# Prompt attention: exponentials read the statistics tile, ScalarE copies the results

## The chip, the cores and the metric

The kernel runs on one core of a Trainium2 chip. The metric is the device time of one execution in microseconds (us). The engines are TensorE (PE in the profile, PEld for its weight loads), VectorE (DVE), ScalarE (ACT), GpSimd (POOL) and SyncE (SP, which here only issues transfers).

## The reference

One layer of a hybrid decoder for a prompt of 2048 tokens and 8 sample sequences of 8 tokens. What matters here is the softmax attention of the prompt: three groups of 4 heads (head size 64), with dilations 1, 4 and 16; each query sees itself and 128 positions back at its group's stride.

```
s = q k^T / 8 - slope * distance        (masked outside the window)
m = max(s);  p = exp(s - m);  den = sum(p)
o = p v                                  (not yet divided)
```

`m` and `den` are needed later, when the groups are combined with weights equal to their denominators. Before this stage come the projections of the whole input, after it the attention of the samples, a chunked delta rule, two output projections and a layer norm.

## The kernel before

The program is written out engine by engine with semaphores. `attend_prompt` does the prompt attention in 48 units: 3 groups g, each with 16 blocks of 128 queries. A unit has two pairs p of heads, each with two heads h. `x.kb` says over how many blocks of keys a unit runs: 2 in the first group and in three of four units of the second, 1 in the third group and for blocks with no predecessor. In group two tokens are taken with a step of 4, in group three with a step of 16, both in q and k as read by TensorE and in the result tile `att_T` as written.

`schedule` gives every engine the same order of steps; step k handles unit k+1 (`nxt`), k (`now`) and k-1 (`prev`):

- TensorE: `score(nxt)` into `ps_s`; `weigh(prev)`, probabilities times values into `ps_o`, after `t_read` of each pair p and after `o_read` of the unit before; then `transpose(now)` into `ps_t`.
- VectorE: `turn(prev)` copies the transposed probabilities of pair 0 to `probs_T`; `maxima(nxt)` adds the bias, writes `scores` and takes the row maximum into `top` (L1321); two small multiplications by -1 write `neg` (L1326) and `stats` (L1327); `results(prev)` copies `ps_o` to `att_T` (L1332) and posts `o_read`.
- ScalarE: `turn(prev)` for pair 1 (L1367), then `exps(nxt)`: four exponentials with `neg` as bias and the row sum into `stats` (L1361), after `neg_put`.
- SyncE loads the groups' tiles, stores finished rows of `att_T` after `o_read`, and the statistics.

There is one `ps_o` and one `probs_T`, two slots of `scores`, `probs` and `neg`. `att_T` of groups one and three is the same tile; hence a wait for `row_stored[0]` (group one's stores) before group three writes it. In the trace the result tile of group two goes by the name `v_first`, whose place it takes.

The stage after, `attend_samples`, starts on ScalarE with a table load and the activations of the gates (L1770 to L1775); VectorE builds the decay rates from them, and TensorE adds these up (L1577) before it scores the second half of the samples (L1518).

Of the kernel before, what the change touches and what calls it, by code (L numbers as in the profile page):

```python
# [8 lines left out]
ALU = mybir.AluOpType  # L9
# [3 lines left out]
P = 128  # L13
# [9 lines left out]
HPG, DH = 4, 64  # L23
# [1017 lines left out]
def attend_prompt(nc, t, block, first, late, pair, g_last):  # L1041


    with ExitStack() as ctx:
# [12 lines left out]
        probs = sb("probs", [P, 2, NP_, 2, 2 * P])  # L1057
        probs_T = sb("probs_T", [P, NP_, 4, P])
        top = sb("top", [P, HPG])
        neg = sb("neg", [P, 2, HPG])  # L1060
        turnstile = sb("turnstile", [P, NP_])
        ps_s = [[pb(f"ps_s{p}{h}", [P, 512]) for h in range(2)] for p in range(NP_)]
        ps_t = [pb(f"ps_t{p}", [P, 4, P]) for p in range(NP_)]
# [3 lines left out]
        qk_in = [sem(f"qk_in{g}") for g in range(NG)]  # L1067
        v_in = [sem(f"v_in{g}") for g in range(NG)]
        stat_put = sem("stat_put")
        neg_put, o_full, o_read = sem("neg_put"), sem("o_full"), sem("o_read")  # L1070
        s_full = [sem(f"s_full{p}") for p in range(NP_)]
        s_read = [sem(f"s_read{p}") for p in range(NP_)]
        exp_done = [sem(f"exp_done{p}") for p in range(NP_)]
# [231 lines left out]
        @block.vector  # L1305
        def _(dve):
            dve.wait_ge(bias0_in, 16)

            def maxima(x):
                for p in range(NP_):  # L1310
                    dve.wait_ge(s_full[p], x.u + 1)
                    if x.after(2):
                        dve.wait_ge(exp_done[p], 2 * (x.u - 1))
                    if x.after(1):
                        dve.wait_ge(stat_put, x.u)

                    dve.memset(turnstile[:, p:p + 1], 0.0)
                    for h in range(2):
                        head = 2 * p + h
                        off = 2 * P - P * x.kb  # L1320
                        dve.tensor_tensor_reduce(out=scores[:, x.slot, p, h, 0:P * x.kb], in0=ps_s[p][h][:, 0:P * x.kb],  # L1321
                                                 in1=bias[x.g][:, head, off:], scale=DH ** -0.5, scalar=-3.0e38, op0=ALU.add,
                                                 op1=ALU.max, accum_out=top[:, head:head + 1]).then_inc(s_read[p], 1)
                for p in range(NP_):
                    dve.wait_ge(s_read[p], 2 * (x.u + 1))
                dve.tensor_scalar(neg[:, x.slot, :], top[:, :], -1.0, None, ALU.mult).then_inc(neg_put, 1)  # L1326
                dve.tensor_scalar(stats[:, x.g, x.b:x.b + 1, 0:HPG], top[:, :].unsqueeze(1), -1.0, None,  # L1327
                                  ALU.mult).then_inc(stat_put, 1)

            def results(x):  # L1330
                dve.wait_ge(o_full, x.u + 1)
                dve.tensor_copy(x.tokens(att_T[x.g], 0), ps_o[:, :, :]).then_inc(o_read, 1)  # L1332

            def step(nxt, now, prev):
                if prev:
                    turn(dve, lambda o, i: dve.tensor_copy(o, i), 0, prev)
                if nxt:
                    maxima(nxt)
                if prev:
                    results(prev)  # L1340

            def enter(g):
                if g == 2:
                    dve.wait_ge(row_stored[0], 16 * 4)

            def leave(g):
                if g == 0:
                    dve.wait_ge(bias_in, 16)
            schedule(step, enter, leave=leave)

        @block.scalar
        def _(act):

            def exps(x):
                act.wait_ge(neg_put, x.u + 1)
                for p in range(NP_):
                    if x.after(2):
                        act.wait_ge(t_full[p], x.u - 1)
                    for h in range(2):
                        head = 2 * p + h  # L1360
                        act.activation(probs[:, x.slot, p, h, 0:P * x.kb], scores[:, x.slot, p, h, 0:P * x.kb], ACT.Exp,  # L1361
                                       bias=neg[:, x.slot, head:head + 1],
                                       accum_out=stats[:, x.g, x.b:x.b + 1, HPG + head]).then_inc(exp_done[p], 1)

            def step(nxt, now, prev):
                if prev:
                    turn(act, lambda o, i: act.activation(o, i, ACT.Copy), 1, prev)  # L1367
                if nxt:
                    exps(nxt)
            schedule(step)  # L1370


CACHED = sum(KEPT)
# [2786 lines left out]
```

## Time and profile before

| | us |
|---|---|
| median of 3 runs | 2448.22 |
| lowest, highest | 2446.05, 2450.98 |
| span of the profiled execution | 2441.7 |
| TensorE busy in the span | 2332.4 |
| VectorE busy | 1644.5 |
| ScalarE busy | 1165.6 |
| prompt attention, from to | 1414.0 to 1571.7 |

The profiled execution is one run of its own; the profile gives its span, from the first to the last instruction, and no other time for it. What lies around the span is therefore known only as the difference between the median and the span, 6.5 us. In a row of the timeline the first number is the start in us from the span's start, the second the length of the row (which may hold several instructions), and the bracket at its end is the idle time of that engine before it and what ended it; "issue" is a wait for nothing that the profile shows.

### The profile page before, as it was taken

The page shows a single profiled execution, that of the slowest core. Times are in us where ns is not written, and L with a number is a line of the kernel's source. Part 1 is how long each engine was busy: PE and PEld are TensorE (multiplying, and loading weights), DVE is VectorE, ACT ScalarE, POOL GpSimd, SP SyncE. Part 2 cuts the span into 40 slices and gives each one's busy share as a digit, 9 for nine tenths or more (in the row PEclk, how much of TensorE's full clock was granted, in tenths as well). Part 3 has the DMA queues.
Part 4 walks back from the last instruction along what each step waited for, and adds up shares of the span by engine and source line. Part 5 has one row for each costly group of instructions (what it writes and reads, how often), then busy time and mean ns, then how long its engine had stood idle before and what let it go on. Part 6 is the DMA issues. An engine that isn't in the chain of part 4 may idle for free. (4 is left out here: it accounts for less than half of the span.)

```text
span 2441.7 us, 45441 instructions
## 1 busy us (share of the span) xinstructions
PE 2332.4 (96%) x16842; PEld 2056.4 (84%) x16842; DVE 1644.5 (67%) x4158; ACT 1165.6 (48%) x2458; POOL 375.0 (15%) x628
## 2 busy tenths in 40 slices
PE   5999999999999999999999999979999899999998
PEld 2777788888899999999999966648888699999786
DVE  5867676554363776776644467758996877677897
ACT  4444444444431543544444466737776533333454
POOL 0000000000111111110000000222322035345100
PEclk8999999999999999999999999979999699999999
DMA  7232323333532323323333363876666566657563
GB/s 264 95 113 95 113 96 112 104 105 100 192 99 87 93 92 109 98 87 110 108 107 108 109 247 122 306 251 176 164 179 196 175 201 194 200 183 237 184 215 128
DMA packets 246588, 363.59 MB, mean 149 GB/s; under 512 B 48598, under 2 KB 180286, under 8 KB 241120
## 3 DMA queue, kind: packets, MB, share of 16 engines
q1 hardware_dynamic: 187792, 224.11, 29.8%
q0 software_dynamic: 36560, 125.17, 13.4%
q10 hardware_dynamic: 22016, 11.40, 1.7%
q8 instruction: 135, 2.21, 0.4%
q14 instruction: 85, 0.70, 0.1%
HBM read 246.94 MB, written 113.68 MB: 148 GB/s over the span
## 5 line engine op out<-in xcount | busy, mean ns | idle before, releaser
L310 PE MATMUL ps_f<-m_lo,w_hi 128*128 128x272 f32 (+1 forms) x2436 | 789.6, 324 | 13.5 <-DVE m_lo L620 6.9
L310 PE MATMUL ps_f<-m_hi,w_hi 128*128 128x272 f32 (+1 forms) x2436 | 793.4, 326 | 0.0
L310 PE MATMUL ps_f<-m_hi,w_lo 128*128 128x272 f32 (+1 forms) x2436 | 784.7, 322 | 0.0
L310 PEld LDWEIGHTS ps_f<-m_lo,w_hi 128*128 128x128 f32 x2436 | 458.8, 188 | 68.4 <-issue 33.0
L310 PEld LDWEIGHTS ps_f<-m_hi,w_lo 128*128 128x128 f32 x2436 | 459.6, 189 | 36.8
L310 PEld LDWEIGHTS ps_f<-m_hi,w_hi 128*128 128x128 f32 x2436 | 458.7, 188 | 33.7
L684 DVE TENSOR_TENSOR stage<-partial,ps_f 128x512 f32<-128x512 f32 (+2 forms) x348 | 171.4, 506 | 319.0 <-PE ps_f L310 307.5
L435 ACT ACTIVATE partial<-ps_f 128x272 f32<-128x272 f32 (+1 forms) x348 | 161.1, 463 | 392.6 <-PE ps_f L310 390.9
L397 ACT ACTIVATE w_hi<-w_raw 128x512 fp32r<-128x512 f32 x348 | 213.0, 625 | 204.0 <-PE ps_f L310 128.1
L591 DVE TENSOR_TENSOR w_lo<-w_raw,w_hi 128x512 fp32r<-128x512 f32 x348 | 239.1, 688 | 85.0 <-ACT w_hi L397 81.5
L709 DVE SCALAR_TENSOR_TENSOR conv<-stage,side,conv 128x1024 f32<-128x1024 f32 x108 | 138.3, 1281 | 8.1 <-ACT conv L451 6.9
L65 PE MATMUL ps_f<-wv_lo,m_hi 128*128 128x256 f32 (+1 forms) x384 | 109.4, 285 | 4.2 <-DVE wv_lo L751 3.7
L66 PE MATMUL ps_f<-wv_hi,m_lo 128*128 128x256 f32 (+1 forms) x384 | 109.6, 286 | 0.0
L67 PE MATMUL ps_f<-wv_hi,m_hi 128*128 128x256 f32 (+1 forms) x384 | 109.0, 284 | 0.0
L1361 ACT ACTIVATE probs<-scores,neg 128x256 f32<-128x256 f32 (+1 forms) x192 | 86.3, 450 | 45.2 <-DVE neg L1326 45.2
L66 PE MATMUL ps_fm<-u_hi,w_tail_lo 128*128 128x256 f32 (+1 forms) x336 | 97.2, 289 | 0.0
L66 PE MATMUL ps_fm<-u_first_hi,w_tail_lo 128*128 128x256 f32 x336 | 95.0, 283 | 0.0
L898 POOL DMA_DIRECT2D scratch_conv_d<-conv x36 | 19.5, 540 | 431.0 <-ACT conv L457 424.3
L65 PEld LDWEIGHTS ps_f<-wv_lo,m_hi 128*128 128x128 f32 x384 | 73.4, 191 | 4.8 <-DVE wv_lo L751 4.1
L457 ACT ACTIVATE conv<-conv 128x1024 f32<-128x1024 f32 (+1 forms) x36 | 39.1, 1086 | 78.4 <-DVE conv L709 50.6
L67 PEld LDWEIGHTS ps_f<-wv_hi,m_hi 128*128 128x128 f32 x384 | 73.6, 192 | 0.0
L66 PEld LDWEIGHTS ps_f<-wv_hi,m_lo 128*128 128x128 f32 x384 | 73.3, 191 | 0.0
(766 smaller groups left out, 4783.1 us busy)
## 6 DMA issues: line engine op xcount, KB each, us to landing
w_raw<-in_w_feat SPq DMA_DIRECT2D x58, 1024.0 KB, 5.9
gates<-scratch_g_d SPq DMA_DIRECT2D x56, 256.0 KB, 3.2
m_rows<-scratch_parts_d SPq DMA_DIRECT2D x16, 768.0 KB, 5.0
z_f<-scratch_z_d ACTq DMA_DIRECT2D x13, 768.0 KB, 6.7
scratch_conv_d<-conv POOLq DMA_DIRECT2D x18, 544.0 KB, 3.0
scratch_conv_d<-conv POOLq DMA_DIRECT2D x18, 512.0 KB, 2.9
kc<-in_k_cache SPq DMA_DIRECT2D x8, 1152.0 KB, 15.1
vc<-in_v_cache POOLq DMA_DIRECT2D x8, 1152.0 KB, 16.3
```

Of the source, the lines that this page charges most:

```text
L65: pe.matmul(out, ah, bl, start=start, stop=False)
L66: pe.matmul(out, al, bh, start=False, stop=False)
L67: return pe.matmul(out, ah, bh, start=False, stop=stop)
L310: last = pe.matmul(out[:, 0:n], l[:, cols], r, start=start and k == 0 and nth == 0, stop=k == KH - 1 and nth == 2, skip_group_check=not start)
L397: act.activation(wh[j][:, :], source(q, j), ACT.Copy).then_inc(w_hi_done[j], 1)
L435: act.activation(f[:, which, 0:n], src[:, 0:n], ACT.Copy).then_inc(put, 1)
L457: act.activation(conv[:, j, 0:n], conv[:, j, 0:n], ACT.Silu).then_inc(conv_silu, 1)
L591: put(dve.tensor_tensor(wl[j][:, :], source(q, j), f32(wh[j][:, :]), ALU.subtract), w_lo_done[j])
L684: last = dve.tensor_tensor(x[:, S_PRE + HT * h + at:S_PRE + HT * h + at + m], left[:, 0:m], right[:, 0:m], ALU.add)
L709: put(dve.scalar_tensor_tensor(out=conv[:, j, 0:PT], in0=x[:, n:n + PT], scalar=w, in1=conv[:, j, 0:PT], op0=ALU.mult, op1=ALU.add), conv_ ...
L898: pool.dma_start(t["conv_d"][tile(q, j), :, PT * s:PT * s + n], conv[:, j, 0:n]).then_inc(conv_stored[j], 16)
L1361: act.activation(probs[:, x.slot, p, h, 0:P * x.kb], scores[:, x.slot, p, h, 0:P * x.kb], ACT.Exp, bias=neg[:, x.slot, head:head + 1], acc ...
```

## The change

The tile `neg` and its semaphore go. The exponentials wait for `stat_put` and take their bias from `stats`. `results`, with its wait for `o_full`, moves from VectorE's step to the end of ScalarE's step, and with it the wait for `row_stored[0]` before group three.

```diff
-        neg = sb("neg", [P, 2, HPG])
...
-                dve.tensor_scalar(neg[:, x.slot, :], top[:, :], -1.0, None, ALU.mult).then_inc(neg_put, 1)
                 dve.tensor_scalar(stats[:, x.g, x.b:x.b + 1, 0:HPG], top[:, :].unsqueeze(1), -1.0, None,
                                   ALU.mult).then_inc(stat_put, 1)
-
-            def results(x):
-                dve.wait_ge(o_full, x.u + 1)
-                dve.tensor_copy(x.tokens(att_T[x.g], 0), ps_o[:, :, :]).then_inc(o_read, 1)
...
-                if prev:
-                    results(prev)
-
-            def enter(g):
-                if g == 2:
-                    dve.wait_ge(row_stored[0], 16 * 4)
...
-            schedule(step, enter, leave=leave)
+            schedule(step, leave=leave)
 
         @block.scalar
         def _(act):
 
             def exps(x):
-                act.wait_ge(neg_put, x.u + 1)
+                act.wait_ge(stat_put, x.u + 1)
...
-                                       bias=neg[:, x.slot, head:head + 1],
+                                       bias=stats[:, x.g, x.b, head:head + 1],
                                        accum_out=stats[:, x.g, x.b:x.b + 1, HPG + head]).then_inc(exp_done[p], 1)
 
             def step(nxt, now, prev):
...
                 if nxt:
                     exps(nxt)
-            schedule(step)
+                if prev:
+                    results(prev)
+
+            def results(x):
+                act.wait_ge(o_full, x.u + 1)
+                act.activation(x.tokens(att_T[x.g], 0), ps_o[:, :, :], ACT.Copy).then_inc(o_read, 1)
+
+            def enter(g):
+                if g == 2:
+                    act.wait_ge(row_stored[0], 16 * 4)
+            schedule(step, enter)
```

## Rows read from the trace of the kernel before

**Rows 1.** Busy time by head group: stretch, length, engines' busy us, clock.

```profile
1414.00:1467.70 53.70, 52.14 (x468) 37.16 (x468) 42.44 (x223) 40.50 (x143) 0.00 (x0) 0.94 0.74 281
1467.70:1531.00 63.30, 63.30 (x500) 44.45 (x496) 45.42 (x239) 41.08 (x156) 0.00 (x0) 1.00 0.34 128
1531.00:1571.70 40.70, 38.14 (x324) 27.32 (x321) 30.55 (x211) 29.72 (x137) 5.88 (x14) 1.00 0.91 325
```

**Rows 2.** Timeline, first group: start us, length us, engine, work.

```profile
1442.17 0.51 ACT L1361 ACTIVATE probs<-scores,neg 128x256 f32<-128x256 f32 x1 [0.93 <-DVE neg L1326]
...
1444.16 0.57 ACT L1367 ACTIVATE probs_T<-ps_t 128x512 f32<-128x512 f32 x1
...
1444.78 0.42 PEld L1261 LDWEIGHTS ps_o<-probs_T,v_first 128*64 128x64 f32 x8 [0.40 <-ACT probs_T L1367]
...
1445.37 0.86 PEld L1250 LDWEIGHTS ps_t<-ident_top,probs 128*128 128x128 f32 x8 [0.17 <-issue]
...
1446.39 0.73 PEld L1237 LDWEIGHTS ps_s<-k_first,q_first 64*128 64x128 f32 x8 [0.17 <-issue]
...
1447.15 0.42 DVE L1321 CUSTOM_DVE_ANT_0 scores<-ps_s,bias_head 128x256 f32<-128x256 f32 x1 [0.40 <-issue]
...
1448.73 0.17 DVE L1326 TENSOR_SCALAR neg<-top 128x4 f32<-128x4 f32 x1
1448.81 0.16 DVE L1327 TENSOR_SCALAR stats<-top 128x4 f32<-128x4 f32 x1
...
1448.93 0.51 ACT L1361 ACTIVATE probs<-scores,neg 128x256 f32<-128x256 f32 x1 [0.93 <-DVE neg L1326]
```

**Rows 3.** Timeline, third group.

```profile
1534.93 0.40 ACT L1361 ACTIVATE probs<-scores,neg 128x128 f32<-128x128 f32 x1 [0.86 <-DVE neg L1326]
...
1536.90 0.20 PEld L1261 LDWEIGHTS ps_o<-probs_T,v_sb 128*64 128x64 f32 x4 [0.39 <-ACT probs_T L1367]
...
1539.95 0.40 ACT L1361 ACTIVATE probs<-scores,neg 128x128 f32<-128x128 f32 x1 [0.78 <-DVE neg L1326]
```

**Rows 4.** Timeline, second group.

```profile
1494.03 0.57 ACT L1367 ACTIVATE probs_T<-ps_t 128x512 f32<-128x512 f32 x1
...
1494.57 0.85 PEld L1261 LDWEIGHTS ps_o<-probs_T,v_first 128*64 128x64 f32 x16 [0.70 <-issue]
...
1497.77 0.57 ACT L1367 ACTIVATE probs_T<-ps_t 128x512 f32<-128x512 f32 x1
1497.85 0.96 PEld L1261 LDWEIGHTS ps_o<-probs_T,v_first 128*64 128x64 f32 x16 [0.22 <-issue]
```

**Rows 5.** VectorE's result copy: durations ns min/median/max, groups one, two, three.

```profile
L1332 DVE COPY att_T<-ps_o x15: 417/425/426, 1421.8 to 1469.0; 128x256 f32<-128x256 f32 x15
...
L1332 DVE COPY v_first<-ps_o x16: 611/630/647, 1477.0 to 1532.4; 128x256 f32<-128x256 f32 x16
...
L1332 DVE COPY att_T<-ps_o x16: 579/589/597, 1534.9 to 1571.8; 128x256 f32<-128x256 f32 x16
```

**Rows 6.** ScalarE's turn of 128x256: busy us, mean ns, idle before.

```profile
L1367 ACT ACTIVATE probs_T<-ps_t 128x256 f32<-128x256 f32 x21 | 7.6, 363 | 1.1 <-PE ps_t L1250 1.1
```

**Rows 7.** Timeline, two ScalarE copies in a row, next stage.

```profile
1608.52 0.60 ACT L1812 ACTIVATE o_rows_s<-ps_so 128x512 f32<-128x512 f32 x1 [12.45 <-PE ps_so L1554]
1609.01 0.38 ACT L1813 ACTIVATE o_rows_s<-ps_so 128x256 f32<-128x256 f32 x1
```

**Rows 8.** Timeline, the seam to the next stage.

```profile
1571.13 1.28 ACT L1770 ACT_TABLE_LOAD   x1
...
1571.84 0.60 DVE L1332 COPY att_T<-ps_o 128x256 f32<-128x256 f32 x1 [0.84 <-PE ps_o L1261]
...
1577.22 0.30 PEld L1577 LDWEIGHTS ps_G<-coef,tri_incl 128*128 128x128 f32 x2 [0.84 <-issue]
...
1579.49 0.77 PE L1518 MATMUL ps_ss<-k_new,q_bd_s 128*128 128x64 f32 x5 [0.44 <-DVE top_s L1636]
```

**Rows 9.** Busy time in the stage after; columns as in rows 1.

```profile
1587.00:1648.00 61.00, 46.01 (x321) 30.32 (x319) 31.49 (x159) 20.49 (x66) 15.49 (x22) 0.76 0.73 251
```

More of the change, by code:

```diff
@@ L1069, in attend_prompt @@
         stat_put = sem("stat_put")
-        neg_put, o_full, o_read = sem("neg_put"), sem("o_full"), sem("o_read")
+        o_full, o_read = sem("o_full"), sem("o_read")
         s_full = [sem(f"s_full{p}") for p in range(NP_)]
```

## The prediction

> **What bounds the kernel now.** I read the profile from the stage that is changed outwards: first the busy times of the three head groups of the prompt attention, then the chain inside one pair of units in each group, then the seam to the next stage. A unit is one block of 128 queries with 4 heads; there are 48, 16 in each group.
>
> The stage lasts 157.7 us, from 1414.0 to 1571.7, and TensorE is busy nearly all of it; VectorE and ScalarE are each busy about three quarters [rows 1]. That alone would say that a copy may move freely between the two. It is the wrong reading here, because busy TensorE time is pipelined and the question is who releases its next instruction.
>
> In the first group follow one lap [rows 2]. ScalarE starts the exponentials of a unit at 1442.17. After the four of them (1.99 us) it copies half of the transposed probabilities of the unit before (`turn`, L1367) from 1444.16. TensorE's second half of `weigh` waits for that copy, and its weights load at 1444.78, behind an idle 0.40 that ScalarE ends. Then come the transposes (1445.37), the scores of the unit after next (1446.39), VectorE's scaled maxima (1447.15, after 0.40 of idling), the negated maximum (1448.73), and ScalarE again at 1448.93. So the lap takes 6.76 us and carries the even units; the odd ones make the same lap in between. Two units per 6.76 us is 3.38 us a unit, and 16 of them are 54 us, which is the length of the first group [rows 1]. So this ring of latencies sets the pace, and ScalarE's stretch "exponentials, then turn" lies on it without a gap. VectorE lies on it only between its first maximum and the negation; everything else it does falls into time in which it then idles.
>
> In the third group it is the same with shorter tiles: 1534.93 to 1539.95, 5.02 us for two units, with a visible wait of 0.39 for ScalarE's turn [rows 3].
>
> The second group reads its queries and keys with a stride, its score matmuls take longer, and there TensorE's own work sets the pace: it loads weights at 1494.57 without a wait for ScalarE, whose turn is over at 1494.60 [rows 4]. The second half of `weigh` begins some 0.43 later, at 1495.00, so ScalarE has 0.40 to spare. Once in each row of four units the scores are short (a block with no predecessor), and there the turn ends at 1498.34 where the second half would start at 1497.85 + 0.43 = 1498.28: nothing to spare [rows 4].
>
> **The change part by part.**
>
> *One multiplication less on VectorE.* Today `neg` is written at 1448.73 and the same values to `stats` at 1448.81, 0.08 later [rows 2]. After the change the `stats` write comes first and the exponentials wait for it. It takes 0.16 us against 0.17 for `neg`, so ScalarE starts when it did. Gain on the ring: 48 times 0.01 at most, taken as zero. The 0.08 saved behind it is VectorE time ahead of an idle 0.40.
>
> *The result copy leaves VectorE.* It took 0.42 us a unit in the first group, 0.63 in the second and 0.59 in the third [rows 5]. It ran after the negation, while ScalarE was in its exponentials, and was followed by VectorE's turn and then idling before the next maximum. It was on no ring, so its removal gives nothing. If that cover were gone it would be worth 16 x (0.42 + 0.63 + 0.59) = 26 us, but other engines hold the pace long before (rival 2).
>
> *The result copy joins ScalarE, behind the exponentials of the unit after next and ahead of the next turn.* The semaphore it waits for (`o_full`) is up by then: TensorE is past `weigh` at 1445.37, and the exponentials that begin about then take 1.99 us [rows 2]. So it does not wait. But it is queued in front of exactly the copy for which TensorE waits in groups one and three. No row shows this copy on ScalarE. The nearest is its turn of the same 128 x 256 shape from PSUM, 0.36 us [rows 6]. That row writes contiguous rows. In groups two and three the destination steps by 4 and by 16 elements, and there VectorE pays 0.63 - 0.42 = 0.21 and 0.59 - 0.42 = 0.17 more than in group one [rows 5]. I take the same extra for ScalarE: 0.36, 0.57, 0.53. Two ScalarE copies in a row overlap: one of 0.60 us starts at 1608.52 and the next at 1609.01, so 0.11 of each is hidden [rows 7]. What the turn is put back by is then 0.25, 0.46 and 0.42 us.
>
> The ScalarE page of the Trainium skill (ScalarE: Activation LUTs, section "What ACT_TABLE_LOAD costs") gives 186 ns + 0.833 ns an element, 0.40 us here, and an overlap of 93 ns; the turn's 0.36 [rows 6] and the overlap of 0.11 [rows 7] are a little better. By the page each delay would be 0.06 larger, which over the 20 delays below is 1.2 us more. The skill's page on SBUF (SBUF — State Buffer, section "Door 1: The DMA port swizzle") says that accesses which go to a new 16-byte line each time pay a penalty, whatever engine makes them; VectorE's 0.63 and 0.59 agree [rows 5], ScalarE's share is shown by no row. Without any such penalty the sum would be 6.0 instead of 8.3.
>
> Now the sum. First group: the ring of 6.76 grows by 0.25 for every two units, 8 x 0.25 = 2.0 us. Third group: 8 x 0.42 = 3.4 us. Second group: of the four steps of a row only the one with short scores is bare, 4 x 0.46 = 1.8 us; in the others the 0.40 to spare covers most of 0.46, and a delay in one step gives the next one more room. Together 7.2 us. The other new wait, TensorE's first half of `weigh` for `o_read`, now posted by ScalarE at the end of the copy, is met at about the moment at which the turn starts; the first half takes 0.43 and the turn 0.57, so the turn still ends last.
>
> *The seam.* Today ScalarE leaves the stage with its last turn and starts a table load for the next stage at 1571.13, while VectorE copies the last result from 1571.84, when TensorE has finished it [rows 8]. After the change ScalarE must do that copy first, and the load starts near 1571.84 + 0.53 - 0.11 = 1572.26, 1.1 us later against TensorE. Behind it hang the gate exponentials of the next stage, VectorE's work on them, and TensorE, which already idles 0.84 at 1577.22 and 0.44 for VectorE's maxima at 1579.49 [rows 8]. So the 1.1 is passed on. *The wait for `row_stored`* moves from VectorE to ScalarE ahead of group three: group one is over at 1467.7 and group three begins at 1531.0 [rows 1], so stores that follow each row of group one have had 63 us, and it waits for nothing. If they were late, the turns would be held. SyncE's stores of the results wait for `o_read`, which comes up to 2 us later in a unit; nothing reads them before the stage after.
>
> Sum: 7.2 + 1.1 = 8.3 us. The profiled span is 2441.7 us and the median of the three times 2448.2, so 6.5 us lie around the span; I leave them as they are. 2448.2 + 8.3 = 2456.5 us, 0.34% slower. A measurement of this kernel can tell about 0.2% (4.9 us) from no change.
>
> Bounds. Below: no extra for strides, 20 x 0.25 = 5.0 and a covered seam: 2453.2. Above: ScalarE copies in VectorE's times with no overlap, and the ordinary steps of group two show 0.63 - 0.40 once a row: 8 x 0.42 + 4 x 0.86 + 8 x 0.59 + 1.3 = 12.8, giving 2461.0.
>
> **The rivals.**
>
> *Rival 1, it is hidden (same).* The waits for ScalarE are small (0.40, of which 0.17 is also shown where nothing is waited for, and 0.39) [rows 2, 3]. If a queue inside TensorE is the true limit and the ring only looks closed, only the seam is left: 2449.3. Against it: the laps of 6.76 and 5.02 close without a gap.
>
> *Rival 2, VectorE was the pace (not slower).* If the maxima started when VectorE got to them, freeing it would pull the ring in, until TensorE is without waits: 0.40 - 0.17 = 0.23 per pair in group one and 0.39 in group three, 8 x 0.23 + 8 x 0.39 = 5.0 us, so 2443.2 at best. It decides only if VectorE's idle 0.40 ahead of L1321 is not there; the row shows it [rows 2].
>
> *Rival 3, TensorE's clock falls otherwise in the next stage (faster or much slower).* From 1587 to 1648 the granted clock averages 0.76, so for 0.24 / 0.5 x 61 = 29 us the engine is at 1.2 GHz and not 2.4; it is busy in only 46 of the 61 us there [rows 9]. Work that arrives some 8 us later could meet fewer low stretches: if all were gone and TensorE's work there were bare, 15 us come back and the end is 2456.5 - 15 = 2441.5. As well it can meet more of them, and with 10 us more the end is 2466. For it: nothing ties those stretches to our work but its gaps. Against: the gaps are made by that stage's own chain and move with it.
>
> *Rival 4, strided PSUM to SBUF copies are dearer on ScalarE than on VectorE.* Well above 0.40 + 0.11 us group two is exposed in its ordinary steps too: at 1.0 us it is 2.0 + 4 x 0.9 + 12 x 0.5 + 8 x 0.9 + 1.5 = 20 us, 2468. No row speaks for so much.
>
> **How the numbers follow.** Forecast 0.68; rival 1 0.17; faster, by the clock or by rival 2 with the scatter of runs, 0.06; rivals 3 and 4 on the slow side 0.09. The range reaches from rival 1's 2449.5 to a little over the upper bound, 2463.5, which leaves 2 in 10 out; the forecast's own range is 2453 to 2461. Slower by over 0.2%: nearly all of the forecast but its lowest edge, and the slow side of 3 and 4, 0.74. Within 0.2%: rival 1 and that edge, 0.20. Faster 0.06.
>
> **What would show it.** In the profile after: the copy stands between the fourth exponential and the turn, at 0.36, near 0.57 and near 0.53 us; two laps of group one take about 7.0 us and of group three about 5.45; TensorE's wait for ScalarE (or for the copy itself) ahead of `weigh` grows; VectorE idles over 0.8 us a unit; the table load follows the last copy, and TensorE's idle 0.84 at the sums of the gate grows to nearly 2. I am wrong if the laps keep their length, if the copy waits for `o_full`, or if the stage is about 7 us longer and the end does not move.

## The result and the profile after

The changed kernel takes 2453.6 us, the median of 10 runs (2450.8 to 2458.8); the kernel before took 2446.6 us in the 10 runs beside it (2442.0 to 2451.0). The ratio is 1.0032, with an interval of 1.0022 to 1.0041: 0.32% slower, where 0.34% was forecast. Against the median of 2448.2 that the forecast started from, 2456.5 was put at 8.3 us more; against the 2446.6 of the larger sample the ratio gives 7.8 us.

Wherever a run's time stands beside its span, little lies around the span: 1.8 to 1.9 us in the kernel before, 1.7 to 1.8 in the changed kernel, up to 2.2 in some of the runs below. The profiled execution of the kernel before was thus a short one (2441.7 + 1.8 = 2443.5), not one of median length with 6.5 us around it. The spans of the two profiled executions differ by 10.8 us, more than the medians. So I compare the stage, which repeats, and not the spans.

The first group after the change, in the timeline (start, length, engine, work, idle time before and its end):

```profile
1440.81 0.51 ACT L1348 ACTIVATE probs<-scores,stats 128x256 f32<-128x256 f32 x1 [0.93 <-DVE stats L1324]
...
1442.79 0.36 ACT L1362 ACTIVATE att_T<-ps_o 128x256 f32<-128x256 f32 x1
...
1443.06 0.58 ACT L1354 ACTIVATE probs_T<-ps_t 128x512 f32<-128x512 f32 x1
1443.20 0.90 PEld L1260 LDWEIGHTS ps_o<-probs_T,v_first 128*64 128x64 f32 x16 [0.93 <-ACT att_T L1362]
...
1444.27 0.86 PEld L1249 LDWEIGHTS ps_t<-ident_top,probs 128*128 128x128 f32 x8 [0.17 <-issue]
...
1445.30 0.73 PEld L1236 LDWEIGHTS ps_s<-k_first,q_first 64*128 64x128 f32 x8 [0.17 <-issue]
...
1446.06 0.42 DVE L1319 CUSTOM_DVE_ANT_0 scores<-ps_s,bias_head 128x256 f32<-128x256 f32 x1 [0.40 <-issue]
...
1447.84 0.51 ACT L1348 ACTIVATE probs<-scores,stats 128x256 f32<-128x256 f32 x1 [0.93 <-DVE stats L1324]
```

Beside [rows 2] the reader sees the copy of 0.36 us at 1442.79, behind the fourth exponential, and the turn 0.27 later. The lap from exponentials to exponentials is 1447.84 - 1440.81 = 7.03 us; it was 6.76. TensorE's idle before `weigh` is 0.93 and named after the copy itself: it waits for `o_read` at the first half, and the second half no longer waits at all (16 weights in one row). VectorE's step now begins its maxima where it did, relative to the scores.

The third group, against [rows 3]; the lap is 5.47 us and was 5.02:

```profile
1542.29 0.40 ACT L1348 ACTIVATE probs<-scores,stats 128x128 f32<-128x128 f32 x1 [0.37 <-DVE stats L1324]
...
1543.85 0.57 ACT L1362 ACTIVATE att_T<-ps_o 128x256 f32<-128x256 f32 x1
...
1544.24 0.40 ACT L1354 ACTIVATE probs_T<-ps_t 128x256 f32<-128x256 f32 x1
...
1544.48 0.42 PEld L1260 LDWEIGHTS ps_o<-probs_T,v_sb 128*64 128x64 f32 x8 [0.59 <-ACT att_T L1362]
...
1547.76 0.40 ACT L1348 ACTIVATE probs<-scores,stats 128x128 f32<-128x128 f32 x1 [0.37 <-DVE stats L1324]
```

A unit with short scores in the second group, against [rows 4]; the copy takes 0.60 and TensorE, which did not wait there, is idle for 0.78:

```profile
1498.06 0.60 ACT L1362 ACTIVATE v_first<-ps_o 128x256 f32<-128x256 f32 x1
...
1498.45 0.63 ACT L1354 ACTIVATE probs_T<-ps_t 128x512 f32<-128x512 f32 x1
...
1498.71 0.85 PEld L1260 LDWEIGHTS ps_o<-probs_T,v_first 128*64 128x64 f32 x16 [0.78 <-ACT v_first L1362]
```

The seam, against [rows 8]:

```profile
1574.60 0.42 PEld L1260 LDWEIGHTS ps_o<-probs_T,v_sb 128*64 128x64 f32 x8 [1.79 <-ACT att_T L1362]
...
1576.82 1.41 PEld L1515 LDWEIGHTS ps_ss<-k_new,q_bd_s 128*128 128x128 f32 x12 [0.17 <-issue]
...
1576.93 0.60 ACT L1362 ACTIVATE att_T<-ps_o 128x256 f32<-128x256 f32 x1 [0.67 <-PE ps_o L1260]
1577.54 1.28 ACT L1767 ACT_TABLE_LOAD   x1
...
1583.38 0.30 PEld L1574 LDWEIGHTS ps_G<-coef,tri_incl 128*128 128x128 f32 x2 [1.92 <-issue]
...
1585.44 2.33 PEld L1515 LDWEIGHTS ps_ss<-k_new,q_bd_s 128*128 128x128 f32 x12 [0.42 <-DVE top_s L1633]
```

ScalarE copies the last result at 1576.93 and loads its table at 1577.54, 0.72 us behind TensorE's first score of the samples (1576.82); before it was 0.60 ahead of it (1571.13 against 1571.7). TensorE's idle at the sums of the gate is 1.92 us and was 0.84.

The laps and three lengths tell the kernels apart; all are differences of starts in the timelines. "Exponentials" is the time from the first exponential of unit 0 to that of unit 47, "stage" that from TensorE's first score to its first score of the samples, "seam" that from there to the sums of the gate.

| kernel | lap, group 1 | row of 4 units, group 2 | lap, group 3 | exponentials | stage | seam | time against before (interval) |
|---|---|---|---|---|---|---|---|
| before | 6.76 | 15.03 | 5.03 | 151.4 | 157.7 | 5.5 | |
| after | 7.03 | 15.60 | 5.46 | 158.3 | 164.9 | 6.6 | 1.0032 (1.0022 to 1.0041) |
| neg removed only | 6.76 | 15.03 | 5.03 | 151.1 | 158.0 | 5.6 | 0.9997 (0.9981 to 1.0013) |
| copy moved only | 7.03 | 15.60 | 5.46 | 158.2 | 165.1 | 8.3 | 1.0040 (1.0026 to 1.0053) |
| VectorE relieved, ScalarE not loaded | 6.76 | 15.02 | 5.03 | 151.4 | 159.1 | 5.6 | 0.9998 (0.9987 to 1.0009) |
| after, last two copies on VectorE | 7.03 | 15.60 | 5.46 | 158.3 | 165.9 | 9.0 | 1.0040 (1.0026 to 1.0054) |
| after, one more small copy | 7.11 | 15.78 | 5.55 | 160.1 | 166.8 | 6.7 | one run |
| after, contiguous writes | 7.04 | 15.30 | 5.30 | 156.1 | 163.7 | 6.4 | 1.0026 (1.0014 to 1.0038) |
| after, copy ahead of exponentials | 7.18 | 15.35 | 5.66 | 160.7 | 167.9 | 8.8 | 1.0056 (1.0039 to 1.0072) |
| both turns on VectorE | 6.22 | 14.92 | 4.67 | 144.7 | 155.3 | 7.8 | 0.9985 (0.9971 to 0.9999) |
| the same, samples' queries early | 6.22 | 14.92 | 4.66 | 144.3 | 149.6 | 5.5 | 0.9971 (0.9960 to 0.9983) |
| before, samples' queries early | 6.76 | 15.04 | 5.02 | 151.1 | 157.4 | 5.5 | 0.9994 (0.9983 to 1.0005) |

### The profile page after: what moved, and what is told of

Same layout as the page of the kernel before. It is cut to its first block and busy times, and to the rows that moved or that the text cites. A ratio compares the mean times of both kernels' runs of the same rounds, so it can differ in the third digit from the quotient of the medians.

```text
span 2452.5 us, 45393 instructions
## 1 busy us (share of the span) xinstructions
PE 2340.2 (95%) x16842; PEld 2062.7 (84%) x16842; DVE 1622.8 (66%) x4062; ACT 1184.0 (48%) x2506; POOL 374.0 (15%) x628
## 5 line engine op out<-in xcount | busy, mean ns | idle before, releaser
L1348 ACT ACTIVATE probs<-scores,stats 128x256 f32<-128x256 f32 (+1 forms) x192 | 86.3, 450 | 35.0 <-DVE stats L1324 34.9
L987 DVE TENSOR_TENSOR sub_prod<-sub_u,sub_w 96x60 f32<-96x60 f32 (+34 forms) x434 | 71.7, 203 | 4.0 <-issue 3.6
## 6 DMA issues: line engine op xcount, KB each, us to landing
vc<-in_v_cache POOLq DMA_DIRECT2D x8, 1152.0 KB, 17.5
```

Of the source, the lines that this page charges most:

```text
L987: dve.tensor_tensor(prod[:, rows, 0:m], u[:, i:i + 1, i + 1:].broadcast_to(some), w[:, rows, i:i + 1].broadcast_to(some), ALU.mult).then_i ...
```

## The experiments

### One half each: which edit costs

The first run takes the tile `neg` away and leaves the copy on VectorE:

```diff
-                dve.tensor_scalar(neg[:, x.slot, :], top[:, :], -1.0, None, ALU.mult).then_inc(neg_put, 1)
...
-                act.wait_ge(neg_put, x.u + 1)
+                act.wait_ge(stat_put, x.u + 1)
...
-                                       bias=neg[:, x.slot, head:head + 1],
+                                       bias=stats[:, x.g, x.b, head:head + 1],
```

> The kernel before with one edit only: the tile neg and its multiplication are gone and the exponentials read the statistics tile; VectorE still copies the results. My theory (the ring of latencies): the statistics are written at the moment at which neg was, so nothing moves: two laps of group one stay 6.76 us, of group three 5.02, the stage 157.7 us, the time within 0.1% of before. The rival (VectorE's instructions count one by one): 48 x 0.08 us less, the stage near 154 us.

Measured: laps of 6.76 and 5.03 us, exponentials 151.1 us, ratio 0.9997. The first edit is worth nothing, as its place ahead of an idle VectorE says.

The second run keeps `neg` and moves `results` and the wait for `row_stored[0]` to ScalarE, as in the changed kernel.

> The other half alone: ScalarE copies the results behind the exponentials, neg stays. My theory: the whole loss is here; the stage is as long as with both edits, 164.9 us (before 157.7), laps 7.03 and 5.47 us, and the time about 7 us above before. The rival (the later statistics tile costs something, or the two edits work against each other): the stage differs from 164.9 by over 1 us.

Measured: 7.03 and 5.46 us, stage 165.1, ratio 1.0040. Every lap is that of the changed kernel. The whole loss is in the move of the copy.

### VectorE without the copy, ScalarE without it

```diff
-                dve.tensor_copy(x.tokens(att_T[x.g], 0), ps_o[:, :, :]).then_inc(o_read, 1)
+                if x.u == 0:
+                    dve.wait_ge(att_clear, 1)
+                n = P if x.g == 1 else 2
+                dve.tensor_copy(x.tokens(att_T[x.g], 0)[:, :, 0:n], ps_o[:, :, 0:n]).then_inc(o_read, 1)
```

> VectorE is relieved and ScalarE is not loaded: as the run with neg removed, but in groups one and three VectorE copies 2 of 128 columns of each result, so the results of these groups are left out (GpSimd clears their tile once at the start of the stage; group two copies in full). My theory (VectorE's copy lies under ScalarE's exponentials): the stage stays 157.7 us within 1 us. The rival (VectorE was the pace): the laps of groups one and three shrink by up to 0.23 and 0.39 us, the stage is up to 5 us shorter.

The laps do not move (6.76, 5.03), the exponentials take 151.4 us as before, and the ratio is 0.9998. In the timeline of this run the short copy is followed by a turn that waits for TensorE:

```profile
1440.87 0.16 DVE L1335 COPY att_T<-ps_o 128x4 f32<-128x4 f32 x1
...
1441.36 0.69 DVE L1339 COPY probs_T<-ps_t 128x512 f32<-128x512 f32 x1 [0.34 <-PE ps_t L1251]
```

The 0.42 us taken away from VectorE came back as waiting for the transposes and for the scores. The stage, expected within 1 us of 157.7, is 1.4 us longer, but not in the laps: 1.3 of it lie ahead of the first exponential, where one write of the statistics takes 1.45 us while GpSimd's added clearing runs. So rival 2 is out: VectorE was not the pace, and its relief was worth nothing to begin with.

### The price per ScalarE time

```diff
+                act.activation(junk[:, :], ps_o[:, 0, 0:32], ACT.Copy)
                 act.activation(x.tokens(att_T[x.g], 0), ps_o[:, :, :], ACT.Copy).then_inc(o_read, 1)
```

> The changed kernel with one more small ScalarE copy (128 x 32 from the same PSUM tile to a spare tile) ahead of each result copy. My theory (every bit of ScalarE time between exponentials and turn is paid once per lap in groups one and three and once per row of four in group two): about 0.1 us of queue time x 20 delays, so the stage goes from 164.9 to about 167 us, a little more if the ordinary steps of group two are bare by now. The rival (ScalarE idles 0.4 to 0.9 us a unit and takes it for nothing): 164.9.

A lap grows by 0.08 and 0.09 us, a row by 0.18, the exponentials by 1.8 us and the stage by 1.9. That is 8 x 0.08 + 8 x 0.09 + 4 x 0.18 = 2.1 us by the laps. A row of group two pays 0.18, twice the price and not once, as if two of its steps were bare with the copy in them. (Its one time, 2453.0 us, cannot tell 2 us.)

```diff
-                act.activation(x.tokens(att_T[x.g], 0), ps_o[:, :, :], ACT.Copy).then_inc(o_read, 1)
+                act.activation(att_T[x.g][:, :, P * x.b:P * (x.b + 1)], ps_o[:, :, :], ACT.Copy).then_inc(o_read, 1)
```

> The changed kernel, but ScalarE writes each result to contiguous columns of its tile and not with the group's step, so the results of groups two and three lie in the wrong columns. My theory: the copy takes 0.36 us in all groups instead of 0.61 and 0.58; laps of group three near 5.3 us instead of 5.47, rows of group two 0.4 us shorter; the stage about 162.8 us. The rival (the longer copies come from reading PSUM while TensorE works with long strided matmuls, not from the step of the write): 0.6 us remain and 164.9.

The copy's durations (ns, min/median/max, groups one and three, then group two):

```profile
L1362 ACT ACTIVATE att_T<-ps_o x32: 357/362/386, 1423.4 to 1577.4; 128x256 f32<-128x256 f32 x32
L1362 ACT ACTIVATE v_first<-ps_o x16: 359/362/363, 1480.5 to 1536.3; 128x256 f32<-128x256 f32 x16
```

With contiguous writes every copy takes 0.36 us, where the changed kernel's took 0.60 in group two and 0.58 in group three. So the step of the write is what costs, 0.24 and 0.22 us a copy, and the rival (TensorE's strided matmuls) is out. Laps of group three shrink from 5.46 to 5.30 and rows of group two from 15.60 to 15.30: the exponentials take 156.1 us, 2.2 less. The stage is 163.7 us, 0.9 over what was expected of it; that part lies behind the last exponentials (5.4 us from there to the samples' scores, 4.4 in the changed kernel), where the granted clock is 0.50 from 1574 to 1577 and was 1.00 in the changed kernel.

### Another place for the copy on ScalarE

```diff
+                if prev:
+                    results(prev)
                 if nxt:
                     exps(nxt)
-                if prev:
-                    results(prev)
```

> The changed kernel with ScalarE's result copy ahead of the exponentials of its step and not behind them. There ScalarE idles 0.45 to 0.93 us before, so a count of idle time says: hidden, the stage is near 158 us. My theory says no: the copy must wait for the weighing, which waits for ScalarE's turn, so a ring of one step closes: turn 0.57 + weighing 0.65 + copy 0.27 + exponentials 1.98 = 3.5 us a unit in group one (as now) and 0.36 + 0.45 + 0.49 + 1.55 = 2.85 in group three (2.73 now): the stage about 166 us, not shorter than the changed kernel.

The idle time ahead of the exponentials was no free place: the ratio is 1.0056, the laps 7.18 and 5.66 us, and the stage 167.9 us, 2 more than expected. In group three one reads the ring of one step: weights after the turn, copy after the weighing, exponentials after the copy, turn after the exponentials:

```profile
1545.62 0.37 ACT L1354 ACTIVATE probs_T<-ps_t 128x256 f32<-128x256 f32 x1
...
1546.04 0.20 PEld L1260 LDWEIGHTS ps_o<-probs_T,v_sb 128*64 128x64 f32 x4 [0.52 <-ACT probs_T L1354]
...
1546.53 0.60 ACT L1362 ACTIVATE att_T<-ps_o 128x256 f32<-128x256 f32 x1 [0.54 <-PE ps_o L1260]
...
1546.94 0.36 ACT L1348 ACTIVATE probs<-scores,stats 128x128 f32<-128x128 f32 x1
...
1548.46 0.36 ACT L1354 ACTIVATE probs_T<-ps_t 128x256 f32<-128x256 f32 x1
```

The turn starts at 1545.62, the copy at 1546.53 and the next turn at 1548.46: the ring closes in 2.84 us a unit, half of 5.66. Group two, paced by TensorE, is indeed a little better off here (15.35 against 15.60).

### The seam alone

```diff
+                if prev and prev.u >= 46:
+                    dve.wait_ge(o_full, prev.u + 1)
+                    dve.tensor_copy(prev.tokens(att_T[prev.g], 0), ps_o[:, :, :]).then_inc(o_read, 1)
...
-                if prev:
+                if prev and prev.u < 46:
                     results(prev)
```

> The changed kernel with the copies of the last two units given back to VectorE. My theory of the seam: ScalarE's table load for the next stage starts 1.1 us earlier against TensorE, and from the end of the last weighing to TensorE's sums of the gate it is 5.5 us again and not 6.6; the stage itself keeps 164.9 us less some tenths. The rival (the seam is set by something else): 6.6 us remain. Whether the 1.1 us reach the end of the kernel is open: in the profile of the changed kernel the stage behind had given them back some 65 us later; if so, the time is that of the changed kernel.

```profile
1577.21 1.28 ACT L1770 ACT_TABLE_LOAD   x1
1578.00 2.63 PEld L1518 LDWEIGHTS ps_ss<-k_new,q_bd_s 128*128 128x128 f32 x12 [0.33 <-issue]
...
1578.11 0.59 DVE L1334 COPY att_T<-ps_o 128x256 f32<-128x256 f32 x1 [1.30 <-PE ps_o L1260]
...
1587.02 0.30 PEld L1577 LDWEIGHTS ps_G<-coef,tri_incl 128*128 128x128 f32 x2 [0.84 <-issue]
```

The table load comes 0.79 us ahead of the samples' scores again, and TensorE's idle at the sums is 0.84 again: this much of the mechanism of the seam is as described. But the length came out at 9.0 us and not 5.5, for a reason that neither theory had: here TensorE runs at the lower clock. (A later run, with both turns on VectorE as well, has the same last two copies at a clock of 1.00, and there the seam is 5.5 us.) Twelve weight loads took 2.63 us, where the changed kernel's took 1.41. In its profile, in that with only the copy moved (8.3 us) and in that with the copy ahead (8.8 us), the granted clock falls to 0.50 at the seam. In this profile TensorE has just idled 1.79 us before the weighing of unit 46, where it must wait for a copy that stands behind the last four exponentials, and 0.55 before that of 47. The first wait is new; the changed kernel has it too. In the changed kernel's own profile the clock held at the seam and fell right behind it (2.33 us for the next twelve weights at 1585.44). Whether the 1.1 us of the seam reach the end could not be told from the times: 1.0040 against the changed kernel's 1.0032, with intervals that overlap.

The starts of VectorE's instructions tell how far it goes, if they are counted from the stage's first score and not from the start of the span, from which that score lies 0.5 to 2.2 us less far in these profiles than in the one before (1414.1). The instruction that starts at 1597 before is then 10.2 us late with only the copy moved, 6.7 with contiguous writes and 11.7 with the last copies on VectorE; stage and seam together are 10.2, 6.9 and 11.7 us longer. So as far as 1597 the seam is passed on whole, within 0.3 us. In the changed kernel's profile the same count gives 11.4 us where stage and seam make 8.4. The other 3.0 us fall where its granted clock is 0.50, from about 1586 to 1592; in the kernel before it is 1.00 from 1571 to 1597.

### Opening the ring

If ScalarE's stretch "exponentials, copy, turn" is the ring, then ScalarE may have the copy if it loses the turn.

```diff
                     turn(dve, lambda o, i: dve.tensor_copy(o, i), 0, prev)
+                    turn(dve, lambda o, i: dve.tensor_copy(o, i), 1, prev)
...
-                if prev:
-                    turn(act, lambda o, i: act.activation(o, i, ACT.Copy), 1, prev)
+                if prev:
+                    results(prev)
                 if nxt:
                     exps(nxt)
-                if prev:
-                    results(prev)
```

> The changed kernel with both turns on VectorE, and ScalarE's result copy ahead of its exponentials. My theory: this opens the ring, because the exponentials no longer have a turn behind them; TensorE's own 3.27 and 2.33 us a unit are left: laps of 6.54 and 4.66 us, the stage 4 to 5 us shorter than before, 153 to 154.5 us, and the time some 0.15% below before. The rival (VectorE, at two turns and the maxima some 3.1 us a unit, becomes the pace, or its later maxima close another ring): the stage 158 us or longer.

```profile
1441.73 0.68 DVE L1330 COPY probs_T<-ps_t 128x512 f32<-128x512 f32 x1
...
1442.34 0.42 DVE L1319 CUSTOM_DVE_ANT_0 scores<-ps_s,bias_head 128x256 f32<-128x256 f32 x1
...
1442.52 0.85 PEld L1260 LDWEIGHTS ps_o<-probs_T,v_first 128*64 128x64 f32 x16 [0.33 <-issue]
...
1443.66 0.39 ACT L1361 ACTIVATE att_T<-ps_o 128x256 f32<-128x256 f32 x1 [0.56 <-PE ps_o L1260]
...
1443.91 0.17 DVE L1324 TENSOR_SCALAR stats<-top 128x4 f32<-128x4 f32 x1
1444.12 0.51 ACT L1349 ACTIVATE probs<-scores,stats 128x256 f32<-128x256 f32 x1
```

Now the weights of `weigh` load 16 in a row with nothing before them but the 0.33 of changing from scores, ScalarE is idle before its copy, and VectorE goes from turn to maxima without a pause. The lap of group one is 6.22 us, less than the 6.54 that I had called TensorE's own: that figure still held the gap between the two halves of `weigh`. Together the exponentials take 144.7 us, 6.7 less than before. But the stage is only 2.4 us shorter (155.3, where 153 to 154.5 was expected), and the timeline says why:

```profile
1564.79 4.95 POOL L1221 TENSOR_SCALAR q_bd_s<-q_s 64x64 f32<-64x64 f32 x12 [34.97 <-DMA bias_s<-in_bias_samples]
...
1569.79 2.64 PEld L1514 LDWEIGHTS ps_ss<-k_new,q_bd_s 128*128 128x128 f32 x12 [5.47 <-POOL q_bd_s L1221]
```

TensorE arrived 5.47 us before GpSimd had the samples' queries in place, and that work (4.95 us) had waited for the last of five small loads. It had always ended near there; in the kernel before TensorE happened to come 0.3 us behind it. The next run lets GpSimd start as soon as the queries themselves have landed, and gives the last two copies to VectorE:

```diff
-                sp.dma_start(late["q_in"][:, :, :], ...).then_inc(late["small_in"], 16)
+                sp.dma_start(late["q_in"][:, :, :], ...).then_inc(late["q_landed"], 16)
...
-            pool.wait_ge(late["small_in"], 80)
+            pool.wait_ge(late["q_landed"], 16)
...
             pe.wait_ge(q_put, 1 + 4 * NG)
+            pe.wait_ge(small_in, 64)
```

> The kernel with both turns on VectorE and the copy ahead of the exponentials, with two more edits: VectorE copies the results of the last two units, and GpSimd prepares the samples' queries as soon as these have landed (a semaphore of their own) and not after all five small loads, for which TensorE waits itself. In the run before this one the stage's laps were 6.7 us shorter in sum but TensorE then waited 5.2 us for GpSimd's product, which stood behind the last of those loads. My theory: with that wait gone the stage keeps its gain, about 151 us from the first score to the first score of the samples (before 157.6), no idle time for GpSimd's tile, TensorE's idle at the sums of the gate 0.84 as before; the time 5 to 7 us below before. The rival: the samples' keys and the bias land late as well, so another wait, for a transfer, takes the place, and the gain stays at 2 to 3 us.

```profile
1562.69 1.42 PEld L1518 LDWEIGHTS ps_ss<-k_new,q_bd_s 128*128 128x128 f32 x12 [0.17 <-issue]
...
1568.18 0.30 PEld L1577 LDWEIGHTS ps_G<-coef,tri_incl 128*128 128x128 f32 x2 [0.84 <-issue]
```

The wait is gone (0.17 before the samples' weights), the stage is 149.6 us, the seam 5.5, and the time 2439.9 us against 2446.2: ratio 0.9971, interval 0.9960 to 0.9983. It beats both kernels. The same edit alone, beside the removal of `neg`:

> The kernel before without neg, and with GpSimd's early preparation of the samples' queries alone. There GpSimd was ready 0.3 us before TensorE came, so my theory gives nothing: stage 157.6 us, time as before within 0.1%. If it gains, that wait was on the path already.

Stage 157.4 us, ratio 0.9994: nothing, as expected. The gain belongs to the open ring, and the early queries only let it pass.

### Where the lead of the faster kernel goes

The stage is 8.1 us shorter, the time 6.3, and the one profiled execution is not shorter at all (span 2442.7). To see where a lead goes I take the starts of the same VectorE instructions in two profiles. The table gives how much later (+) or earlier (-) than in the profile of the kernel before they start, each counted from the start of its span; its columns are the start there, to a few us.

| kernel | 1597 | 1618 | 1672 | 1895 | 1988 | 2006 | 2398 |
|---|---|---|---|---|---|---|---|
| turns on VectorE, queries early | -9.0 | -4.8 | -5.0 | -3.1 | -1.4 | +0.1 | +1.0 |
| the same, systems' stores ahead | -7.7 | -5.5 | -1.7 | +0.1 | +0.2 | +0.2 | +0.4 |
| the same, values behind stores | -8.6 | +0.3 | -0.4 | +5.1 | +4.7 | +6.2 | +4.8 |
| neg removed only | -0.1 | -0.1 | -1.4 | -1.9 | -0.9 | +0.6 | +1.2 |
| after | +9.3 | +5.3 | +4.4 | +6.8 | +8.6 | +10.0 | +10.8 |
| copy moved only | +8.1 | +8.0 | +8.2 | +10.7 | +11.0 | +13.6 | +14.7 |
| after, contiguous writes | +6.2 | +4.7 | +3.2 | +8.7 | +9.4 | +9.4 | +9.5 |

The first loss, 4.2 us, has a place. (Counted from the stage's first score the lead is 8.1 us at 1597, all that stage and seam gave, and 3.9 at 1618.) VectorE's elimination of the next stage waits for `sub_u`, which takes its way through DRAM; this is its first instruction in the kernel before:

```profile
1617.83 0.19 DVE L987 TENSOR_TENSOR sub_prod_s<-sub_u,sub_w 96x31 f32<-96x31 f32 x1 [18.17 <-issue]
```

In the faster kernel, first GpSimd, which issues the loads of the value cache and must wait for the stores of the results in between; TensorE's wait (the kernel has it wait for these values there, the profile names no releaser); then VectorE's first elimination; then the stores of `UA_first` ahead of it (count, KB each, median us to landing):

```profile
1585.63 1.05 POOL L1476 DMA_DIRECT2D vc<-in_v_cache  x2 [12.06 <-DMA scratch_att_d<-att_T]
...
1596.03 0.50 PEld L1551 LDWEIGHTS ps_so<-v_new,new_T_s 64*128 64x128 f32 x2 [7.12 <-issue]
```

```profile
1613.05 0.19 DVE L987 TENSOR_TENSOR sub_prod_s<-sub_u,sub_w 96x31 f32<-96x31 f32 x1 [22.43 <-issue]
```

```profile
scratch_u_d<-UA_first SPq DMA_DIRECT2D x4, 24.0 KB, 13.8
scratch_u_d<-UA_first POOLq DMA_DIRECT2D x4, 24.0 KB, 16.1
```

VectorE idles 22.4 us where it was 18.2: the difference is the lost lead. The stores of 24 KB take 13.8 and 16.1 us, in the kernel before 12.1, and in both the DMA engines are full (shares of 1.00 to 1.03 in each slice of 4 us from 1588 to 1604). The changed kernel meets the same wait from the other side: it comes 9.3 us late and idles 14.3, its stores landing in 9.5 and 8.6 us, so 3.9 of its delay are swallowed there. That is not so in every run: with only the copy moved the stores take 12.1 and the wait 18.1 us, and 0.1 is swallowed. Two runs were to say which of the two waits, VectorE's or TensorE's, holds the lead. The first puts the loads of sequences 5 to 7 behind the stores of `UA_first`:

```diff
-            values(5, 6, 7)
             for c in range(2):
                 pool.wait_ge(masked, 3 * c + 3)
                 for dst, src in system_blocks(t, c, UA[:, c], 1):
                     pool.dma_start(dst, src).then_inc(u_out[1], 16)
+            values(5, 6, 7)
```

> The faster kernel (both turns on VectorE, the samples' queries early), and GpSimd issues the last three loads of the value cache behind the stores of UA_first and not ahead of them. Theory A (the lead is lost in VectorE's wait for sub_u: the stores of UA_first take 13.8 and 16.1 us to land behind eight loads of 1152 KB, and VectorE idles 22.4 us before its first elimination, 18.2 in the kernel before): with three loads fewer ahead of them, 3 x 1.18 MB at some 420 GB/s = 8 us, the stores land up to 8 us earlier, VectorE's idle falls from 22.4 to 15 to 18, the first elimination starts at 1605 to 1609 instead of 1613.0, and the time is 4 to 7 us less than the faster kernel's, ratio 0.994 to 0.9955. Theory B (the lead is lost in TensorE's wait of 7.12 us for the cached values): that wait stays, the second half of the values comes later, and the time stays or grows, ratio 0.997 to 1.000.

```profile
scratch_u_d<-UA_first SPq DMA_DIRECT2D x4, 24.0 KB, 9.8
scratch_u_d<-UA_first POOLq DMA_DIRECT2D x4, 24.0 KB, 6.8
```

```profile
1612.29 0.44 DVE L987 TENSOR_TENSOR sub_prod_s<-sub_u,sub_w 96x31 f32<-96x31 f32 x1 [20.29 <-DMA sub_u<-scratch_u_d]
```

The stores land in 9.8 and 6.8 us and the idle time is 20.3; of the lead, 2.1 us are lost here and not 4.2. But TensorE waits 9.1 us for the first values (they came 3.4 us later in this profile), the lead is down to 1.7 us at 1672, and the time is 2443.7 against 2448.1: ratio 0.9975 (0.9963 to 0.9987), no better than 0.9971. The second run lets the results' stores land first:

```diff
-            values(2, 3, 4)
             pool.wait_ge(late["stats_out"], 16 * 6)
             for g in range(NG):
                 pool.wait_ge(late["rows_out"][g], 16 * 4)
-            values(0, 1)
+            values(0, 1, 2, 3, 4)
```

> The faster kernel, and GpSimd waits for the stores of the results before it issues the first three loads of the value cache, so that these stores do not share the DMA engines with them; then it issues the loads of sequences 0 to 4. Theory B (TensorE's wait of 7.12 us for the cached values): the stores land some 8 us after their issue at 1571 and not 14.6, the loads of sequences 0 and 1 go out near 1579 instead of 1585.6, TensorE's wait shrinks to 0 to 4 us, and the time is 3 to 6 us less than the faster kernel's, ratio 0.9945 to 0.996. Theory A (VectorE's wait for sub_u): TensorE's wait may shrink, but the same bytes are still ahead of the stores of UA_first, the first elimination starts within 1 us of 1613.0, and the ratio stays at 0.997.

```profile
scratch_u_d<-UA_first SPq DMA_DIRECT2D x4, 24.0 KB, 12.5
scratch_u_d<-UA_first POOLq DMA_DIRECT2D x4, 24.0 KB, 21.8
```

GpSimd goes on at 1583.6, not 1579, all five loads then go out together, TensorE's wait is 8.5 us, and the stores of `UA_first` take up to 21.8. VectorE starts its elimination 0.3 us late against the kernel before, and the ratio is 0.9986 (0.9976 to 0.9996). So neither theory's remedy paid, and neither theory had its numbers right: theory A had the elimination start at 1605 to 1609 in the first run (1612.3) and within 1 us of 1613.0 in the second (1618.1); theory B had TensorE wait 0 to 4 us in the second (8.5). What the runs show is that the start of the elimination moves with the landing of its stores, as theory A has it, and that the 0.8 us which it gained in the first run were no gain further on: the lead at 1672 is 1.7 us there and 5.0 in the faster kernel. That the bytes of this stretch are its bound, and not the order of the loads, fits this but is not shown.

The rest of the lead goes piece by piece further on, partly in stretches with a low clock: from 1900 to 1950 the granted clock is 0.57 in the faster kernel and 0.66 in the kernel before. The table shows as well that the profile of the kernel before is a fortunate one: ten of the thirteen others lose 1.4 to 2.6 us against it between 1988 and 2006, whatever their edit. Hence the medians, and not the spans, carry the verdicts.

## Why the prediction was right, point by point

**The mechanism.** Right in the main, and tested from both sides. The ring of latencies through ScalarE sets groups one and three: loading ScalarE there lengthens the laps, relieving VectorE does not shorten them, and taking the turn out of the ring shortens both. `neg` is worth nothing.

**The terms.** Group one: 0.27 a lap measured, 0.25 forecast. Group three: 0.43 to 0.45 against 0.42. Group two: 0.57 a row against 0.46. 8 x 0.27 + 8 x 0.44 + 4 x 0.57 = 8.0 us by the laps; the stage grew by 7.3 and the exponentials by 6.9, since a lap's delay is not yet there at the edges of the groups; forecast 7.2. The seam: 1.1 and 1.1.

**The sum, and what of it was luck.** 8.3 us were forecast, the ratio gives 7.8. Stage and seam grew by 8.4, so the terms of the sum are borne out. But between them and the end the changed kernel's profile has two terms that the forecast did not list: 3.0 us of lower clock behind the seam, and 3.9 us swallowed in VectorE's wait for `sub_u`. They nearly cancel there (7.5 us are left at 1618, counted from the stage's first score). With only the copy moved it is 10.1 at that place. That the end came out so near the sum is in part luck.

**The duration that no row showed.** 0.36, 0.57 and 0.53 were taken for ScalarE; it took 0.36, 0.60 and 0.58. The step of the write costs ScalarE slightly more than VectorE (0.24 and 0.22 against 0.21 and 0.17), and contiguous writes remove it. The rule that the prediction cites from the Trainium skill (SBUF — State Buffer, section "Door 1: The DMA port swizzle") is stated for accesses to a new 16-byte line without naming an engine, and both engines' numbers agree with it. The overlap, 0.11 for all copies in the forecast, is not one number either: the turn starts 0.27 us behind the start of a contiguous copy and 0.39 behind that of a strided one, so the overlaps are 0.09 and about 0.2, and the turn was put back by 0.39 and not by 0.46 and 0.42.

**What was not seen.** In groups one and three I had the turn end last and the first half of `weigh` just covered. It is the other way round: `weigh` starts at the end of the copy, does its weights in a row, and the turn is done in time. In group three the lap so grew by 0.44, although the turn was put back by only 0.39; the forecast's 0.42 came near by another link of the ring than the one it named. Ahead of the weighing of unit 46 there is a wait of 1.79 us that I did not list. And the 6.5 us around the span were 1.8; since I took them over unchanged, only the explanation was wrong, not the difference.

**The rivals.** Rival 1 (hidden; its end is 2449.3 by its own sum, the 2449.5 in the range is a slip) fell with the laps of the changed kernel and with the extra copy, rival 2 with the relieved VectorE. Rival 3, the clock, is real at the seam, where a fall lengthens it by 1.7 to 3.5 us (8.3 and 8.8 against 6.6, and 9.0 against 5.5), and 3.0 us of it lie behind the seam in the changed kernel's own profile; how much of it the medians hold is not shown, since the wait for `sub_u` can swallow more than that. Rival 4 did not occur at its price, 0.6 us is not 1.0, but its exposure of group two did in part (0.57 a row, and twice the price of the extra copy).

**Left open.** How much of the seam's 1.1 us reaches the end: it is passed on as far as 1597, and the wait for `sub_u` behind that swallowed 3.9 us in one profile and 0.1 in another. Where the faster kernel's lead goes behind 1672. And how much of the difference between the runs at 1.0032 and 1.0040 is the clock at the seam: the intervals hold both.

## What to carry to other kernels

Ask not which engine has idle time but which instruction ends the wait of the busiest one, and follow that chain around once: a copy put on an engine with 25% idle lengthened each lap by 0.27 to 0.44 us, because it stood between two links of the ring, while 0.4 us taken from an engine outside the ring gave nothing. Moving a link out of the ring was worth more than moving load between engines. And when a stage gets shorter, look at once at what the next one waits for: here a product that had been 0.3 us early held back two thirds of the gain, and behind it a wait for stores on full DMA engines took 4.2 us of the lead of 8.1. Starts in two profiles should be compared from the start of the stage in question: what lies ahead of it differed here by up to 2.2 us.

## What the hardware showed that was not expected

A ScalarE copy of 128 x 256 f32 from PSUM takes 0.36 us with contiguous writes and 0.60 and 0.58 us when it writes every 4th or 16th element; the same copy on VectorE took 0.42, 0.63 and 0.59 [rows 5]. So the step brings both engines to nearly one duration. The next ScalarE copy starts 0.27 us behind the start of a contiguous one and 0.39 behind that of a strided one.

TensorE's granted clock fell to 0.50 (1.2 GHz) at the seam in several profiles: with only the copy moved and with the last copies on VectorE, after idling 1.69 and 1.79 us and then 0.60 and 0.55; with the copy ahead of the exponentials, after 1.22 and 0.55; with both turns on VectorE, after 5.47. It held at 1.00 (2.4 GHz) through the seam of the changed kernel, which has idle times of 1.79 and 0.60 too, and fell there only near 1586; with the extra small copy, and the same two idle times, it stayed at 1.00 to 1600. So nearly the same program fell in some profiles and not in others.

Eight stores of 24 KB took 6.8 to 21.8 us (medians of a queue) to land beside loads of 1152 KB that took 13.3 to 17.5: on full DMA engines a small store on the way of a chain can be as late as a large load.
